# Two projection units moved out of the query and key rotations into the banded attention of block 1

## The reference

```python
h = _rms_norm(x, in_norm_g[l])
y = h @ w_in[l] + b_in[l]
(mq, mk, mv, mo, mi, mf, hq, hf, hi, hg, sq, sk, sv) = _split_cols(y, IN_SPLITS)
# mLSTM over (mq, mk, mv, mi, mf), gated by sigmoid(mo)
# HGRN2 over (hq, hf, hi): h_h
h_out = _head_rms_norm(h_h, hgrn_norm_g[l], HGRN_HEADS) * jax.nn.silu(hg)
q_s = _partial_rope(_rms_norm(_heads(sq, 8), swa_q_norm_g[l]), cos, sin)
k_s = _partial_rope(_rms_norm(_heads(sk, 2), swa_k_norm_g[l]), cos, sin)
s_out = swa_sink_attention(q_s, k_s, _heads(sv, 2), swa_sinks[l])
x = x + jnp.concatenate([m_out, h_out, s_out], axis=-1) @ w_out[l]
```

## Time and profile before

| | us |
|---|---|
| median of three runs | 3289.41 |
| the runs | 3280.26, 12733.15, 3289.41 |
| the profiled execution | 3277.75 |
| span in its profile | 3275.9 |
| PE busy (share of the span) | 3130.1 (96%) |
| DVE busy | 1814.8 (55%) |
| ACT busy | 1267.7 (39%) |
| POOL busy | 286.6 (9%) |

### The profile page before, as it was taken

The page is one execution under the profiler, slowest core; times in us unless marked ns, Lnnn a source line. Parts: engine busy times, 40 slices in busy tenths (PEclk is TensorE's granted clock), DMA queues, the critical chain, the costliest instruction groups (busy, mean ns, idle before and its releaser), DMA issues.

```text
span 3275.9 us, 38024 instructions
## 1 busy us (share of the span) xinstructions
PE 3130.1 (96%) x14954; PEld 2469.3 (75%) x14954; DVE 1814.8 (55%) x2626; ACT 1267.7 (39%) x2013; POOL 286.6 (9%) x216
## 2 busy tenths in 40 slices
PE   7898999999999999999998999999999989899998
PEld 5577888887677888886666867888766678678886
DVE  6665644457755643467665645443567646454444
ACT  5645422236644422344444333222334433332222
POOL 2000100011000100011001300000100013000001
PEclk9998999999998999999999999999999989999998
DMA  3110333322111233322112312233211123123322
GB/s 132 45 52 27 96 97 97 96 97 80 49 46 42 93 97 98 98 94 73 53 52 81 125 40 76 97 97 97 84 58 52 46 80 126 46 72 98 97 98 80
DMA packets 73726, 259.12 MB, mean 79 GB/s; under 512 B 8021, under 2 KB 10201, under 8 KB 73177
## 3 DMA queue, kind: packets, MB, share of 16 engines
q1 hardware_dynamic: 72824, 252.99, 24.1%
q0 software_dynamic: 736, 3.87, 0.3%
HBM read 254.73 MB, written 2.10 MB: 78 GB/s over the span
## 4 chain that ended last, share of the span: by engine, by line
PE 86%; DVE 8%; ACT 2%; issue 2%; DVEq 1%; POOLq 0%; DMA 0%; ACTq 0%; POOL 0%
PE bank L501 70%; PE bank L1013 2%; DVE w_lo L1903 1%; PE bank L1024 1%; PE bank L726 1%; PE bank L1034 1%; PE bank L596 1%; PE bank L1038 1%; PE bank L584 1%; PE bank L1050 1%; ACT w_hi L1254 1%; PE bank L765 1%; PE bank L970 1%; PE bank L528 1%; PE bank L753 1%
## 5 line engine op out<-in xcount | busy, mean ns | idle before, releaser
L501 PE MATMUL bank<-a_hi,w_hi 128*128 128x512 f32 x2296 | 928.3, 404 | 41.8 <-DVE w_lo L1903 15.2
L501 PE MATMUL bank<-a_lo,w_hi 128*128 128x512 f32 x2296 | 901.7, 393 | 0.0
L501 PE MATMUL bank<-a_hi,w_lo 128*128 128x512 f32 x2296 | 901.4, 393 | 0.0
L1903 DVE TENSOR_TENSOR w_lo<-w_raw,w_hi 128x1024 fp32r<-128x1024 f32 (+1 forms) x474 | 610.8, 1289 | 284.9 <-ACT w_hi L1254 283.7
L1254 ACT ACTIVATE w_hi<-w_raw 128x1024 fp32r<-128x1024 f32 (+1 forms) x474 | 494.5, 1044 | 440.9 <-DMA w_raw<-weights 440.8
L501 PE MATMUL bank<-b_hi,w_hi 128*128 128x512 f32 (+1 forms) x1432 | 543.5, 380 | 16.0 <-DVE w_lo L1903 8.3
L501 PEld LDWEIGHTS bank<-a_hi,w_hi 128*128 128x128 f32 x2296 | 436.4, 190 | 155.0 <-issue 47.4
L501 PE MATMUL bank<-b_lo,w_hi 128*128 128x512 f32 (+1 forms) x1432 | 535.1, 374 | 0.0
L501 PE MATMUL bank<-b_hi,w_lo 128*128 128x512 f32 (+1 forms) x1432 | 534.4, 373 | 0.0
L501 PEld LDWEIGHTS bank<-a_lo,w_hi 128*128 128x128 f32 x2296 | 436.5, 190 | 94.8 <-issue 7.9
L501 PEld LDWEIGHTS bank<-a_hi,w_lo 128*128 128x128 f32 x2296 | 435.8, 190 | 94.2
(11 more groups left out here) (293 smaller groups left out, 3080.4 us busy)
## 6 DMA issues: line engine op xcount, KB each, us to landing
w_raw<-weights SPq DMA_DIRECT2D x458, 512.0 KB, 3.5
w_raw<-weights SPq DMA_DIRECT2D x16, 384.0 KB, 3.0
x<-x SPq DMA_DIRECT2D x8, 256.0 KB, 7.6
mem<-mem POOLq DMA_DIRECT2D x2, 1024.0 KB, 5.1
out<-x SPq DMA_DIRECT2D x8, 256.0 KB, 2.0
mem<-mem SPq DMA_DIRECT2D x1, 1024.0 KB, 12.5
ple<-ple POOLq DMA_DIRECT2D x2, 512.0 KB, 3.8
o<-c_level SPq DMA_DIRECT2D x1, 512.0 KB
```

What stands on the lines that cost most here:

```text
L501: last = mm(bank[unit_bank(u) if at is None else at][:, 0:cols], w[:, u % SLOTS, ks], t[:, k, 0:cols], start=(k == 0 and n == 0), stop=(k ...
L1903: tt(w_lo[:, u % SLOTS, w], w_raw[:, u % SLOTS, w], f32(w_hi[:, u % SLOTS, w]), ALU.subtract).then_inc(w_lo_ready, 1)
```

## The change

The four halves of units 21 and 22 go from between the rotations into steps 1, 2, 5 and 6 of the attention, behind each step's transposes. Their banks are now 6 and 7 in place of 1 and 0. Spreads of the rotations use banks 7 and 0 in turn and rotations banks 6 and 1, so that each may run one ahead of DVE. Since the unsplit activations' operand tiles are now read during the attention, the probabilities and their transposes can't lie over them: they go to `y[1:12]`. On ACT, `finish(21)` and the weights' high part of unit 25 stand in step 4, `finish(22)` and unit 26 in step 8. On DVE, the evictions stand in steps 3 and 7, the low parts and the products with the silu tiles in steps 5 and 9. HGRN2's norm sums move from bank 6 to 7.

```diff
-        s_prob_t = outer("s_prob_t", [P, 2, ST, 4, P], 0)
-        s_prob = outer("s_prob", [P, 4, 2 * P + 16], 16)
+        s_prob_t = y[:, 1:9, :].rearrange("p (a q) (i b) -> p a q i b", a=2, i=4)
+        s_prob = y[:, 9:12, :].rearrange("p a b -> p (a b)")[:, 0:4 * (2 * P + 16)].rearrange("p (a b) -> p a b", a=4)
...
+            if u - first >= T_HG:
+                return 6 + (u - first) - T_HG
             return 5 if u - first == 4 else W_BANK[(u - first) % 2]
+
+        ROPE_SPREAD, ROPE_TURN = (7, 0), (6, 1)
...
-                def spread(column, b, recip):
+                def spread(column, b, recip, open_=1):
                     n = turn_of["spread"] + 9 * l
                     pe.wait_ge(g_recip, recip)
-                    if n > 0:
-                        pe.wait_ge(g_applied, n)
+                    if n - open_ + 1 > 0:
+                        pe.wait_ge(g_applied, n - open_ + 1)
...
+                def window_spread(j):
+                    if j == 1:
+                        pe.wait_ge(bank_free, first + T_HG)
+                    spread(8 * j, ROPE_SPREAD[j % 2], 3 * l + 2, 2 if j else 1)
+
                 def rotate(j):
                     pe.wait_ge(g_applied, 9 * l + 2 + j + 1)
-                    if j:
-                        pe.wait_ge(g_sin, 5 * l + j)
-                    mm(bank[6][:, :], rot, y[:, (T_SQ, T_SQ + 1, T_SQ + 2, T_SQ + 3, T_SK)[j], :],
+                    if j > 1:
+                        pe.wait_ge(g_sin, 5 * l + j - 1)
+                    mm(bank[ROPE_TURN[j % 2]][:, :], rot, y[:, (T_SQ, T_SQ + 1, T_SQ + 2, T_SQ + 3, T_SK)[j], :],
...
-                spread(0, 7, 3 * l + 2)
+                window_spread(0)
                 level_scores(8)
-                half()
-                spread(8, 7, 3 * l + 2)
+                window_spread(1)
                 rotate(0)
-                half()
-                spread(16, 7, 3 * l + 2)
+                window_spread(2)
                 rotate(1)
                 level_scores(9)
-                half()
-                spread(24, 7, 3 * l + 2)
+                window_spread(3)
                 rotate(2)
-                half()
-                spread(32, 7, 3 * l + 2)
+                window_spread(4)
                 rotate(3)
                 rotate(4)
                 level_sums()
...
+                    if s in (1, 2, 5, 6):
+                        half()
...
+                    if s == 4:
+                        pe.wait_ge(g_applied, 9 * (l + 1))
                     if s == 8:
-                        pe.wait_ge(g_applied, 9 * (l + 1))
                         window_outputs(0)
...
                     window_copy(s)
+                    if s in (4, 8):
+                        finish(T_HG + (0, 1)[s == 8])
+                        ahead(first + 24 + (1, 2)[s == 8])
                     if s + 2 < 16:
                         window_exps(s + 2)
...
-                evict(21)
-                ahead(first + 24)
-                apply_window(1)
+                apply_window(2)
                 rope_sin(1)
-                apply_window(2)
                 rope_add(0)
+                apply_window(3)
+                rope_sin(2)
+                rope_add(1)
                 level_take(9)
-                rope_sin(2)
-                apply_window(3)
-                rope_add(1)
-                evict(22)
+                apply_window(4)
                 rope_sin(3)
-                apply_window(4)
                 rope_add(2)
-                ahead(first + 25)
                 rope_sin(4)
                 rope_add(3)
                 rope_add(4)
-                ahead(first + 26)
+                ahead(first + 24)
...
                     if s in (3, 4):
-                        if s == 3:
-                            dve.wait_ge(t_made, made + T_HG + 2)
                         apply_levels(s - 3)
+                    if s in (3, 7):
+                        evict(T_HG + (0, 1)[s == 7])
+                    if s in (5, 9):
+                        ahead(first + 24 + (1, 2)[s == 9])
+                        gate_levels((0, 1)[s == 9])
```

More of the change, by code:

```diff
@@ L747, in level_sums, with norm_sums @@
                     last.then_inc(h_summed, 1)
-                def norm_sums(tiles, done):
+                def norm_sums(tiles, done, b=6):
                     pe.wait_ge(g_sq, done)
@@ L752, in norm_sums @@
                         for tb in range(ST):
-                            last = mm(bank[6][:, 8 * j + 2 * tb:8 * j + 2 * tb + 2], y[:, t, qs(tb)], halves[:, 18:20],
+                            last = mm(bank[b][:, 8 * j + 2 * tb:8 * j + 2 * tb + 2], y[:, t, qs(tb)], halves[:, 18:20],
                                       start=True, stop=True)
                     last.then_inc(g_nsum, 1)
-                def spread(column, b, recip):
+                def spread(column, b, recip, open_=1):
                     n = turn_of["spread"] + 9 * l
                     pe.wait_ge(g_recip, recip)
-                    if n > 0:
-                        pe.wait_ge(g_applied, n)
+                    if n - open_ + 1 > 0:
+                        pe.wait_ge(g_applied, n - open_ + 1)
                     for tb in range(ST):
@@ L781, in window_scores @@
                         pe.wait_ge(h_taken, 32 * (l + 1))
-                    elif s == 1:
-                        pe.wait_ge(bank_free, first + WIN_T)
-                    else:
+                    elif s > 1:
                         pe.wait_ge(a_exp, 2 * (n - 1))
@@ L801, in window_turn @@
                         for i in range(len(tiles_back(q))):
-                            last = pe.transpose(bank[4 + s % 2][:, qs(2 * e + i)], s_prob[l][:, 2 * (s % 2) + e, qs(i)], ident)
+                            last = pe.transpose(bank[4 + s % 2][:, qs(2 * e + i)], s_prob[:, 2 * (s % 2) + e, qs(i)], ident)
                     last.then_inc(a_turned, 1)
@@ L807, in window_outputs @@
                     pe.wait_ge(g_v, 5 * l + 5)
+                    pe.wait_ge(bank_free, first + WIN_T)
                     if m:
@@ L815, in window_outputs @@
                                     last = mm(half_of(bank[6 + e], half_)[:, qs(q)], v[:, kt, V_SV + 64 * e:V_SV + 64 * e + 64],
-                                              s_prob_t[l][:, half_, q, 2 * e + i, :], start=(i == 0), stop=(i == len(back) - 1))
+                                              s_prob_t[:, half_, q, 2 * e + i, :], start=(i == 0), stop=(i == len(back) - 1))
                         last.then_inc(a_out, 1)
@@ L1475, in squares, with roots @@
                         f(y[:, t, :], src, ACT.Square).then_inc(g_sq, 1)
-                def roots(n, at, columns):
+                def roots(n, at, columns, b=6):
                     act.wait_ge(g_nsum, 3 * l + n + 1)
-                    f(g_r[:, at:at + columns], bank[6][:, 0:columns], ACT.Sqrt, bias=eps, scale=1.0 / 64).then_inc(g_root, 1)
+                    f(g_r[:, at:at + columns], bank[b][:, 0:columns], ACT.Sqrt, bias=eps, scale=1.0 / 64).then_inc(g_root, 1)
                 def window_exps(s):
@@ L1488, in window_exps @@
                         i = (2 * n + e) % 8
-                        f(s_prob[l][:, 2 * (s % 2) + e, 0:nk], bank[2 * (1 - s % 2) + e][:, 0:nk], ACT.Exp, bias=stat_n[:, i:i + 1],
+                        f(s_prob[:, 2 * (s % 2) + e, 0:nk], bank[2 * (1 - s % 2) + e][:, 0:nk], ACT.Exp, bias=stat_n[:, i:i + 1],
                           scale=-1.0, accum_out=stat_d[:, i:i + 1]).then_inc(a_exp, 1)
@@ L2189, in apply_levels, with gate_levels @@
                     stt(t, bank[7][:, :], col("h_g", l, j), t, ALU.mult, ALU.mult).then_inc(g_applied, 1)
-                    dve.drain()
+                def gate_levels(j):
+                    dve.wait_ge(t_made, made + T_HG + j + 1)
+                    t = o[:, 2 + j, :]
                     tt(t, t, y[:, T_HG + j, :], ALU.mult).then_inc(g_o, 1)
@@ L2196, in rope_sin @@
                         dve.wait_ge(g_roped, 5 * l + j - 1)
-                    tt(r_t1[:, j % 2, :], bank[6][:, :], sin_t[:, :], ALU.mult).then_inc(g_sin, 1)
+                    tt(r_t1[:, j % 2, :], bank[ROPE_TURN[j % 2]][:, :], sin_t[:, :], ALU.mult).then_inc(g_sin, 1)
                 def rope_add(j):
```

20 lines of the change are left out of this document (8 added, 12 removed).

## The result

The changed kernel takes 3288.7 us (median of 20 runs), the kernel before 3279.12 in the 20 runs beside it. The ratio is 1.0029, interval 1.0021 to 1.0036: slower by about 9.6 us. One run of each is an outlier (12733.15 and 7368.23 us) and is left out of the ratio.

A forecast was written before the change was run, and what follows sets the result against it. PE was taken to bound the kernel (busy 96% of the span, 86% of the chain). Terms of +4.35 us in the first layer and +1.35 in the second gave +5.7 on 3277.75, 3283.5, put at 3285; range 3266 to 3300.

The forecast's parts named there:

- The wait before the fifth rotation: On PE in the rotations: the fifth rotation waits 3.5 us for DVE's fifth scaling, which stands behind the level copies.
- the wait before step 12's scores: In step 10 of the attention: PE waits about 4 us for ACT's exponentials; priced at +4.5, bounds +2.5 and +5.5.
- the low clock in steps 0 and 1: Start of the attention: clock at 0.50, so the first half takes 5.4 us, +2.4; bounds 0 and +4.9.
- 0.50 from step 10: Attention's tail: clock at 0.50 from step 10 to the end, +3.0 us in the first layer, 0 in the second.
- the rotations' term: First spread to level sums: 16.7 us in place of 31.35, so -14.65 a layer, 11.8 halves and some 2.9 waiting.
- The clock: At the level sums behind the rotations: a clock fall priced at +1.2 us, a third; bounds 0 and +3.7.
- The gain from the clock's earlier return: Attention from step 2's scores: a dense half brings the clock back, 10.8 us becoming 5.9, so -4.9.
- The second part of a table switch: Rival, on ACT in steps 4 and 8: each pair of table loads hides another 1.28 us, +10, 3295; chance 8%.
- The rule cited: Trainium skill page on ACT_TABLE_LOAD: a table switch also costs a drain of about 1.38 us, 2.66 in all.
- The rotations don't close up: Rival, at the rotations: POOL or DVE paces them, the 2.9 us of waiting saved a layer falls away, 3291; chance 10%.
- The clock neither held: Rival: clock keeps 1.00 from the level sums to the attention's end, -10.6 us a layer against forecast, 3264; chance 12%.
- stayed low: Rival: clock stays low from the wait before the fifth rotation to the attention's end, +10.7 us a layer, 3306; chance 15%.

## Why the prediction was right or wrong

**Right: where the time goes.** The wait before the fifth rotation (forecast 3.5, measured 2.96 us, put down to DVE's scaling; that they are so close is in part luck, as PE came there 2.0 us and DVE's scaling 1.5 us later than summed), the wait before step 12's scores (about 4, 4.11), the low clock in steps 0 and 1, 1.00 from the second half on, 0.50 from step 10: all seen. Their causes held when each was taken away: the table loads (2.85 us of 4.11) and the clock in the first steps. Weights were never waited for at the output product.

**Wrong: the size, +5.7 against +9.6 us.** The step that failed is the rotations' term, -14.65 with +1.2 for the clock. It measured -10.3 in both layers, 3.1 us short in each, and 6.3 us together are three quarters of the 8.4 by which the two stages of the profiles exceed the sum. Three things in it were priced too low.

- *A rotation on PE* was taken at 0.56 us, half of a row with two records in 1.13. Both records are of one rotation, and from its start to the next instruction's it takes 1.05 (218.60 to 219.65). Two rotations stand ahead of the third, whose sine product began 11.3 us behind the first spread (225.90) where 10.4 was summed: 0.9 us.
- *The sum on DVE*, at 0.6, takes 1.25 beside POOL's product, and one of them is on the path: 0.6 us, which is what the fifth rotation gained when that product was left out. Together with the rotations this puts the fifth rotation 16.3 us behind the first spread in both layers, in place of 14.8.
- *The clock* I let fall only in the level sums and priced at a third. It fell with the wait in both layers: in the first the fifth rotation itself took twice as long, and the level sums took 6.31 and 7.16 us for 4.50, +1.8 and +2.7. With the rotation that is some 2.7 us a layer, 1.5 more than taken. A bound of +3.7 was on paper; the value was chosen too low in it.

**Smaller misses.** In the first layer the attention cost 2.0 us more than summed: the clock dipped once more behind the wait of 1.30 us, and the fourth half took 4.2 us in place of 2.95; the transposes of step 10 to the last outputs took 14.4 us, 3.8 more than before where 3.0 was taken. In the second layer it cost 1.3 less. The last outputs ran at 0.50 for longer (5.29 and 5.67 us for 4.83), and from them to the output product it took +0.5 and +0.8 us, a term I had at nothing. The gain from the clock's earlier return was about right: from step 2's scores to step 4's, less the half between, 5.2 us where it was 9.7, so -4.5 for -4.9.

**The rivals.** The second part of a table switch didn't come: ACT's silu starts 0.02 us after the load of 1.28, and the wait before step 12 lost 2.85 us with two loads, not twice that. The rule cited isn't borne out by these rows. "The rotations don't close up" was more than half true: the stretch to the level sums shortened by 12.1 and 12.9 us, 11.8 of them the halves, so of the 2.9 us of waiting only 0.3 and 1.1 were saved. One bank again lost 0.6 and 1.4 us of stretch and nothing in the median, and another order on DVE only moved the wait. The clock neither held nor stayed low; it did what the forecast said, but for a dearer fall at the rotations and one more dip.

**Where the expected gain went.** Moving 11.8 us of dense work out of the rotations saves 10.3 there, since DVE's list was just hidden behind it, and costs more than its length in the attention (19.8 and 13.5 us), because its silus came as two switches of tables behind ACT's copy and its first half stood behind the light work that had already brought the clock down. That both are placements is shown: with the two mended the move gains (0.9953), and with half of it undone more (0.9928; the two intervals touch, the medians are 6.2 us apart). What the kernel before would gain from the same two placements with its halves left where they were wasn't tried.

## What to carry to other kernels

In this kernel dense work was cover for another engine's list and for the clock. Before moving it, add up the list it covers; leave there as much as that list lasts beyond PE's own, and put the rest where PE waits with light work ahead, not behind. A function that needs another table goes where ACT waits, once, and not behind the instruction that ends its wait.

## What the runs showed that I had not expected

A DVE sum of two tiles in SBUF goes from 0.68 to 1.25 us while POOL multiplies beside it; the product of a bank with the sine table, run beside POOL's products too, keeps its 0.69. Both slow sums end 0.54 to 0.55 us behind POOL's product (223.70 behind 223.15, 227.76 behind 227.22), and with the level copies late one that began at 225.04, with the product ending at 225.39, took only 0.90 us and ended 0.55 behind it: a slow sum looks like a short one that had to wait for the product's end. The Trainium skill, page "GPSIMD Engine Reference", says in its table of properties that POOL shares its SBUF interfaces with DVE, with contention for instructions that have two SBUF inputs; the traces agree. The level copies took 2.53 us for four beside a POOL product and 2.57 without one in the kernel before. And executions of the changed kernel, but for the outlier, lie between 3285.17 and 3291.8 us; that the place of the clock's falls makes this scatter is likely from the profiles, where one layer dips and the other doesn't, but wasn't tried. A term of one or two us a layer thus shows in the stretch's own rows, hardly in medians of a dozen runs, whose intervals reach some 4 us either way, and not in one span.
